# Two-block transformer step on one core: late expert rows set aside early in memory, with three smaller moves to GpSimd and SyncE

## The chip, the cores and the metric

The kernel runs on one core of a Trainium2 chip. Five engines take instructions: TensorE (PE; PEld loads its weights), VectorE (DVE), ScalarE (ACT), GpSimd (POOL) and SyncE (SP, which here issues most DMAs). The metric is the device time of one launch in microseconds, lower is better.

## The reference

Two transformer blocks follow each other on 2048 tokens of 1024 features, all in float32. The first has latent attention beside a state-space layer. The second has attention beside retention, and then a mixture of 32 experts of which each token takes two. The parts that the change touches compute this:

```python
mixed = jnp.concatenate([attn, ssm], axis=-1) @ w_out[l]
x = x + _rms_norm(mixed, post_norm_g[l])                       # end of block 1 (mixing 1)
...
cross = jnp.einsum('bhnik,nbhkv,hi->bhniv', qc, s_prev, xi)    # retention: queries times a decay xi
...
pcounts = (counts + MOE_BLOCK - 1) // MOE_BLOCK * MOE_BLOCK    # rows of each expert, up to a multiple of 128
buf_tok = jnp.full((P,), T, jnp.int32).at[dest].set(tok_s)     # token of each row
xb = h_pad[buf_tok].reshape(nblk, MOE_BLOCK, D)                # the rows, in blocks of 128
def expert_block(args):
    x_blk, e = args
    return (jax.nn.silu(x_blk @ w_gate[e]) * (x_blk @ w_up[e])) @ w_down[e]
yb = lax.map(expert_block, (xb, blk_e)).reshape(P, D)
```

The rows of an expert are its tokens, gathered from `h`. There are at least 32 blocks of 128 rows (2 x 2048 / 128) and at most 63, since each expert's last block is filled up. With these inputs 46 blocks are used.

## The kernel before

The work runs in stages, each a function with a program for every engine: block 1's attention, state-space layer and mixing (`mix_1`), then projection 2, attention 2, retention, mixing 2, dispatch, experts and combine. The order on each engine is the order in which its program is written; waits on semaphores join the engines. A DMA that SP issues goes on a hardware queue (q1), one that POOL issues as an indirect gather on a software queue (q0).

Experts. A row of this text is the work between the transposes of one block and those of the next. In a row PE transposes the next block's rows (L3766, `e_pT` from `w_XG`), multiplies by gate, up and down weights split in a high and a low part (three products each), and transposes the hidden block. ACT makes the high parts of the weights (L3831), DVE the low parts (L3879: `down_low`, `up_low`, `gate_low`, each 128x4096). SP loads the weights of a block (L3713, 2 MB each; one that has not changed is skipped, so an expert with two blocks loads once) and stores the result (L3717, `between_yb`). In SP's `tile`, the load of gate for block i+2 is the last thing; it waits until `gate_low` has been made. POOL does only one thing: `gather` (L3474) fetches the 128 rows of block i from `between_h` by an indirect DMA, with the list `M["slots"]`, into one of the two buffers `w_XG`, as soon as PE has transposed block i-2 (`t_ps` at i-1):

```python
for i in range(2, NB + 2):
    pool.wait_ge(S["t_ps"], i - 1)
    pool.wait_ge(x_loaded[i % 2], 16 * (i // 2))
    gather(pool, D, M, i)
```

The loop runs over all 64 block numbers, though only some are used: `tiles_in_use` (L82) counts pairs of blocks and skips those not in use, and in a skipped pair SP raises `t_ps` by 2 (`skipped`), which lets POOL run on through the gathers of empty blocks. Their list holds numbers out of bounds, so nothing is fetched. SP also loads the residual (`load_residual`) after the loop. POOL waits for its last gather before the stage ends and combine starts.

Mixing 1. For each of 16 token tiles DVE scales the product (`X`, L1992), later adds the old x to it (`add_x`, L1997), and between them makes `CS` (L2059), from which ACT makes `CH` and then, behind a table load, a tanh that DVE waits for. POOL sums squares of pairs (L1914, L1918), and PE waits for the sum.

Retention. For each of 4 heads DVE runs 15 steps of the state (L3086), makes `QX`, the queries times their decay (`queries`, L3098), and then the decayed scores (L3103) from products of PE. POOL clears memory and is then free.

Of the kernel before, what the change touches and what calls it, by code (L numbers as in the profile page):

```python
# [80 lines left out]

def tiles_in_use(eng, least, most, pairs_in_use, body, skipped_pair=None):  # L82

    body(tile_at(0))
    body(tile_at(1))
    pairs = eng.value_load(pairs_in_use, min_val=least, max_val=most)
    with eng.Fori(0, most) as j:
        with eng.If(j < pairs):
            body(Tile(2 * j + 2, 0, j + 1))
            body(Tile(2 * j + 3, 1, j + 1))  # L90
        if skipped_pair:
            with eng.Else():
                skipped_pair(j)
    return pairs
# [1764 lines left out]
def mix_1(nc, I, D, C, M):  # L1859
# [7 lines left out]
    with ExitStack() as ctx:  # L1867
# [40 lines left out]
        @block.gpsimd  # L1908
        def _(pool):
            k.clear_spent(pool)  # L1910

            def tile(t):
                pool.wait_ge(S["sq_ready"], t.i + 1)
                pool.tensor_tensor(sq_pairs[:], sq[:, 0:SM // 2, :], sq[:, SM // 2:SM, :], ALU.add).then_inc(S["sq_halved"], 1)  # L1914
                pool.wait_ge(S["sq_halved"], t.i + 1)
                if not t.first:
                    pool.wait_ge(S["norm_ps"], t.i)
                pool.tensor_tensor(sq_sum[:], sq_pairs[:, 0, :], sq_pairs[:, 1, :], ALU.add).then_inc(S["sq_summed"], 1)  # L1918

            tiles(pool, NT, tile)  # L1920

        @block.sync
# [56 lines left out]
        def _(dve):  # L1979
# [13 lines left out]

            def add_x(t):
                dve.wait_ge(S["tmp_ready"], t.i + 1)
                dve.wait_ge(x_loaded[t.b], 16 * t.n + 16)
                dve.tensor_tensor(X1[t.b][:], X1[t.b][:], XT[t.b][:], ALU.add).then_inc(S["x1_ready"], 1)  # L1997

            def gelu_inner(t):
# [20 lines left out]
            def tile(t):  # L2020
# [57 lines left out]
            last_stage(tile_at(NT - 1))  # L2078
            add_x(tile_at(NT - 1))

# [494 lines left out]
def attention_2(nc, I, C, D, M):  # L2575
# [14 lines left out]
    with ExitStack() as ctx:  # L2590
# [22 lines left out]
        names = """v_loaded v_ones k_zeros k_rows k_split k_high q_zeros q_high_act q_top q_high q_split max_ps maxed top_ready row_ps row_ready  # L2613
            v_high v_low p_high p_low p_low_dve s_ps p_ready o_ps rec_ready o_ready zeros_ready yb_zeroed
            decay_loaded expo_loaded neg_ready e_ready l_ready lg_ready cols_ready decay_ready decay_step""".split()
# [6 lines left out]
        @block.sync  # L2622
        def _(sp):
            def load_query(i):
                src = D["qka"][0:QA, :].rearrange("(h p) t -> p h t", p=HD)[:, :, i * P:(i + 1) * P]
                for half in range(2):
                    sp.dma_start(RQ[i % 2][half * HD:(half + 1) * HD], src).then_inc(q_loaded[i % 2], 16)

            def load_keys(g):
                for half in range(2):  # L2630
                    sp.dma_start(KX[g][half * HD:(half + 1) * HD, :], D["qka"][QA + g * HD:QA + (g + 1) * HD, :]).then_inc(k_loaded[g], 16)

            load_query(0)
            load_keys(0)
            load_keys(1)
            for g in range(HKV):
                sp.dma_start(V1[:, :, g, 0:HD], D["va"].rearrange("(n p) d -> p n d", p=P)[:, :, g * HD:(g + 1) * HD]).then_inc(S["v_loaded"], 16)
            load_query(1)
            sp.dma_start(ecol[:], I["ret_ecol"]).then_inc(S["expo_loaded"], 16)
            sp.dma_start(expo[:], I["ret_expo"]).then_inc(S["expo_loaded"], 16)  # L2640
            sp.dma_start(R["KT0"][:].rearrange("p n d -> p (n d)"), D["krt"][0:P, :]).then_inc(R["keys_loaded"], 16)
            sp.wait_ge(S["zeros_ready"], 1)
            for n in range(SURE, NB + 1):
                sp.dma_start(D["yb"][n * P:(n + 1) * P, :], zeros[:]).then_inc(S["yb_zeroed"], 16)
            for i in range(NT):
                if i + 2 < NT:
                    sp.wait_ge(S["q_split"], i + 1)
                    load_query(i + 2)
                sp.wait_ge(S["o_ready"], HKV * (i + 1))
                sp.dma_start(D["ao2"].rearrange("(h p) t -> p h t", p=HD)[:, :, i * P:(i + 1) * P], OT[i % 2][:]).then_inc(stored[i % 2], 16)  # L2650
            for b in range(2):
                sp.wait_ge(stored[b], 16 * (NT // 2))
            sp.wait_ge(S["yb_zeroed"], 16 * (NB + 1 - SURE))

# [251 lines left out]
def retention(nc, I, D, C, M):  # L2906

    with ExitStack() as ctx:
# [36 lines left out]
        def _(pool):  # L2945
            pool.memset(K_[HD:P, :], 0.0).then_inc(S["k_zeros"], 1)
            k.clear_spent(pool)

        @block.sync
# [131 lines left out]
        def _(dve):  # L3081
# [10 lines left out]

            def queries(h):
                dve.wait_ge(q_loaded[h % 2], 32 * (h // 2 + 1))
                if h:
                    dve.wait_ge(S["o_ps"], GRP * h)
                q = Q[h % 2][:].rearrange("p (n i) -> p n i", i=P)
                dve.tensor_tensor(QX[:], q, bcast(XI[:, h:h + 1, :], [P, NT, P]), ALU.mult).then_inc(S["qx_ready"], 1)  # L3098

            def decayed(h):  # L3100
# [563 lines left out]
def experts(nc, I, D, C, M):  # L3664

    with ExitStack() as ctx:
# [13 lines left out]
        pD = k.ps("pD", (P, 2, BANK))  # L3680
        names = "turn t_ps xt_high xt_low g_ps u_ps th_ready silu_ready hh_ready ht_ps ht_high ht_low d_ps y_ready".split()
# [3 lines left out]
        x_loaded, stored = M["rows_gathered"], [k.sem(f"stored{b}") for b in range(2)]  # L3685
        block = ctx.enter_context(nc.Block())
# [5 lines left out]
        def after(t):  # L3692
            return Tile(t.i + 1, 1 - t.b, t.n + t.b)

        def raw(n, t):
# [6 lines left out]
        def _(sp):  # L3702
# [44 lines left out]
            wait(w_low["down"], last.i + 1)  # L3747
            for b in range(2):
                wait(stored[b], 16 * pairs + 32)

        @block.gpsimd
        def _(pool):
            k.clear_spent(pool)
            for i in range(2, NB + 2):
                pool.wait_ge(S["t_ps"], i - 1)
                pool.wait_ge(x_loaded[i % 2], 16 * (i // 2))
                gather(pool, D, M, i)
            pool.wait_ge(x_loaded[0], 16 * (NB // 2 + 2))
            pool.wait_ge(x_loaded[1], 16 * (NB // 2 + 1))

        @block.tensor
        def _(pe):
            def transposed(t):
                pe.wait_ge(x_loaded[t.b], 16 * t.n + 16)
                for c in range(KC):
# [32 lines left out]

            def tile(t):
                i = t.i  # L3800
# [5 lines left out]
                if not t.first:  # L3806
                    hidden_transposed(t.before())
                pe.wait_ge(S["xt_low"], i + 1)
                transposed(after(t))
                gate_up(t, pG, "gate", XL, WH)  # L3810
# [9 lines left out]

            pe.sem_inc(S["d_ps"], 1)
            transposed(tile_at(0))
            last = last_in_use(tiles_in_use(pe, *in_use, tile))
            hidden_transposed(last)
# [185 lines left out]
def block_pair_kernel(nc, I, out):  # L4010

    D = {}
    for name, rows, cols in (
# [3 lines left out]
        ("qka", QA + KA, SEQ + CTX), ("qkr", 2 * RQ, SEQ + CTX), ("ao2", QA, SEQ), ("ret", HR * P, NT * RV), ("x2", SEQ, DM),  # L4017
        ("h", SEQ, DM), ("yb", (NB + 1) * P, DM), ("tv", NT * P, GB * POWERS * GC), ("tu", NT * P, GB * POWERS * GC),
        ("w_in_2", DM, PROJ), ("w_out", DM, DM), ("w2h", DM, DM), ("w2l", DM, DM), ("hh", DM, DM * 2), ("hl", DM, DM * 2), ("cos", NT * P, HG * NCH), ("sin", NT * P, HG * NCH),
    ):  # L4020
        D[name] = nc.dram_tensor("between_" + name, [rows, cols], F32, kind="Internal").ap()
    with ExitStack() as ctx:
# [15 lines left out]
        with ExitStack() as projection:  # L4038
# [20 lines left out]
            project_2(nc, I, D, C, M)  # L4059
        M["logits"] = k.sb("logits", [P, NT, NL])  # L4060
        M["weights"] = k.sb("weights", [P, 2, NT])
# [4 lines left out]
        M["pairs_in_use"] = k.sb("pairs_in_use", [P, 1], I32)  # L4066
        M["constants"] = {n: k.sb(n, shape) for n, shape in zip(DISPATCH_CONSTANTS, DISPATCH_SHAPES)}
        M["constants_loaded"] = k.sem("constants_loaded")
# [121 lines left out]
```

## Time and profile before

| what | value |
| --- | --- |
| median of 3 runs | 4377.21 us (4375.51 to 4379.54) |
| the profiled execution: its time, its span | 4377.03 us, 4375.2 us |
| PE, DVE, ACT, POOL busy | 92%, 68%, 56%, 28% of the span |
| mixing 1 | about 1385 to 1668 us |
| retention | about 2997 to 3125 us |
| dispatch ends, experts begin | about 3410 us |
| experts end, combine begins | about 4290 us |

The profile shows one execution. In a timeline row stand the start and the length in us, the engine, the line, the operation, its output and inputs, how many instructions are joined in it, and in brackets how long the engine had been idle before and who released it. SPq and ACTq are DMAs issued on those engines' queues. In a row of windows stand the stretch, its length, the busy time of each engine with its number of instructions, then TensorE's granted clock as a share of full speed, the share of time that the DMA engines were busy, and GB/s.

### The profile page before, as it was taken

The numbers are of one execution on the slowest core, as the hardware profiler recorded it, in microseconds if no ns is written. First come the engines' busy times: TensorE is split into PE (matmuls) and PEld (weight loads), VectorE is DVE, ScalarE is ACT, GpSimd is POOL, SyncE is SP. The second block draws the span as 40 slices with busy tenths as digits, with TensorE's granted clock in tenths as the row PEclk, the third lists the DMA queues.
The fourth block names the chain that finished last, engine by engine and source line by source line (L and its number), as shares of the span: only waits on it lengthen the run. The fifth ranks groups of instructions, "written<-read, shape, count | busy, mean of one in ns | idle before, by whom it ended". The sixth has DMA issues, their size and how long they took to land. (4 is left out here: it accounts for less than half of the span.)

```text
span 4375.2 us, 61240 instructions
## 1 busy us (share of the span) xinstructions
PE 4016.5 (92%) x21445; PEld 3410.6 (78%) x21445; DVE 2986.3 (68%) x3835; ACT 2431.7 (56%) x3867; POOL 1211.5 (28%) x842
## 2 busy tenths in 40 slices
PE   8989799999997997999799999996697799999985
PEld 8978688898776786888588888886586688888872
DVE  6667555555486885444477777775655799999975
ACT  7634333333313554333388888886422577777763
POOL 0000145445310110000288888882000111111114
PEclk9999899999998998999799999998898899999997
DMA  6667733334496433222430000005543688888976
GB/s 229 219 211 243 228 106 118 102 111 124 148 276 189 142 110 114 70 71 72 121 134 15 22 15 15 15 10 181 173 144 111 239 309 327 326 322 337 379 304 276
DMA packets 417337, 728.63 MB, mean 167 GB/s; under 512 B 121744, under 2 KB 314384, under 8 KB 396304
## 3 DMA queue, kind: packets, MB, share of 16 engines
q1 hardware_dynamic: 389040, 665.61, 44.2%
q0 software_dynamic: 13968, 33.58, 2.0%
q10 hardware_dynamic: 14160, 27.27, 2.0%
q8 instruction: 95, 1.56, 0.2%
q14 instruction: 74, 0.61, 0.0%
HBM read 603.93 MB, written 213.91 MB: 187 GB/s over the span
## 5 line engine op out<-in xcount | busy, mean ns | idle before, releaser
L2675 POOL TENSOR_TENSOR a_PL<-a_PT,a_PH 128x512 fp32r<-128x512 f32 x512 | 674.9, 1333 | 132.1 <-ACT a_PH L2794 128.9
L2844 DVE TENSOR_REDUCE a_part<-a_pA 128x1 f32<-128x1024 f32 (+1 forms) x384 | 360.0, 955 | 95.2 <-PE a_pA L2698 90.8
L2792 ACT ACTIVATE a_PT<-a_pB 128x512 f32<-128x512 f32 x576 | 340.8, 592 | 78.6 <-PE a_pB L2721 77.3
L2794 ACT ACTIVATE a_PH<-a_PT 128x512 fp32r<-128x512 f32 x576 | 364.4, 633 | 18.3
L3474 POOL DMA_INDIRECT w_XG<-between_h,all_slots x65 | 119.9, 1845 | 786.6 <-PE e_pT L3766 705.6
L1397 ACT ACTIVATE a_PT<-a_pT 128x512 f32<-128x512 f32 x128 | 69.6, 595 | 408.7 <-PE a_pT L1327 408.7
L1432 DVE TENSOR_REDUCE a_maxima<-a_pS 128x1 f32<-128x512 f32 x256 | 176.1, 689 | 130.0 <-PE a_pS L1309 128.6
L1341 PE MATMUL a_pO<-a_V,a_PT 128*128 128x128 f32 x2048 | 250.4, 276 | 1.0 <-DVE a_PT L1445 1.0
L1341 PEld LDWEIGHTS a_pO<-a_V,a_PT 128*128 128x128 f32 x2048 | 244.2, 192 | 6.8 <-DVE a_PT L1445 1.6
L1239 POOL TENSOR_TENSOR a_QL<-a_RQ,a_QT 128x512 fp32r<-128x512 f32 x16 | 20.6, 1288 | 797.5 <-DVE a_QP L1467 797.5
L2739 PE MATMUL a_pO<-a_PL,a_VH 128*128 128x512 f32 x576 | 225.6, 392 | 3.1 <-DVE a_PL L2854 2.1
L2733 PE MATMUL a_pO<-a_PH,a_VH 128*128 128x512 f32 x576 | 228.1, 396 | 0.0
L2720 PE MATMUL a_pB<-a_QA,a_KH 128*128 128x512 f32 x576 | 225.8, 392 | 1.1 <-ACT a_QA L2767 0.7
L2734 PE MATMUL a_pO<-a_PH,a_VL 128*128 128x512 f32 x576 | 225.8, 392 | 0.0
L2721 PE MATMUL a_pB<-a_QA,a_KL 128*128 128x512 f32 x576 | 225.2, 391 | 0.0
L3879 DVE TENSOR_TENSOR e_gate_low<-w_gate,e_gate_high 128x4096 fp32r<-128x4096 f32 x47 | 207.8, 4421 | 16.1 <-ACT e_gate_high L3831 16.1
L2698 PE MATMUL a_pA<-a_KH,a_QA 128*128 128x512 f32 (+1 forms) x640 | 198.6, 377 | 19.1 <-ACT a_KH L2781 15.6
L3831 ACT ACTIVATE e_up_high<-w_up 128x4096 fp32r<-128x4096 f32 x46 | 167.3, 3638 | 77.0 <-DMA w_up<-in_moe_w_up 69.4
L3879 DVE TENSOR_TENSOR e_down_low<-w_down,e_down_high 128x4096 fp32r<-128x4096 f32 x46 | 203.3, 4419 | 0.8 <-ACT e_down_high L3831 0.7
L3879 DVE TENSOR_TENSOR e_up_low<-w_up,e_up_high 128x4096 fp32r<-128x4096 f32 x46 | 203.1, 4416 | 0.0
L3831 ACT ACTIVATE e_gate_high<-w_gate 128x4096 fp32r<-128x4096 f32 x47 | 170.7, 3632 | 56.1 <-SPq L3721 34.9
L3831 ACT ACTIVATE e_down_high<-w_down 128x4096 fp32r<-128x4096 f32 x46 | 167.3, 3636 | 16.0 <-DMA w_down<-in_moe_w_down 15.8
(651 smaller groups left out, 10601.2 us busy)
## 6 DMA issues: line engine op xcount, KB each, us to landing
w_gate<-in_moe_w_gate SPq DMA_DIRECT2D x48, 2048.0 KB, 7.5
w_up<-in_moe_w_up SPq DMA_DIRECT2D x47, 2048.0 KB, 12.1
w_down<-in_moe_w_down SPq DMA_DIRECT2D x46, 2048.0 KB
between_yb<-e_Y SPq DMA_DIRECT2D x45, 512.0 KB, 7.3
a_row_w<-in_w_ada SPq DMA_DIRECT2D x16, 1024.0 KB, 5.4
between_x<-m_X SPq DMA_DIRECT2D x32, 512.0 KB, 2.7
between_yb<-a_zeros SPq DMA_DIRECT2D x32, 512.0 KB, 14.0
between_tv<-pz_OV SPq DMA_DIRECT2D x16, 576.0 KB, 2.9
```

Of the source, the lines that this page charges most:

```text
L1341: mm = pe.matmul(pO[:, 0:dv], PT[:, jj, :], values(V, h, jj), start=jj == 0, stop=jj == key_tiles - 1)
L2675: pool.tensor_tensor(PL[:, t % RING, :], PT[:, t % RING, :], PH[:, t % RING, :].bitcast(F32), ALU.subtract).then_inc(S["p_low"], 1)
L2720: pe.matmul(pB[t % 2][:], KH[g][:, tile], QA1[i % 2][:, heads, :], start=True, stop=False)
L2721: pe.matmul(pB[t % 2][:], KL[g][:, tile], QA2[i % 2][:, heads, :], start=False, stop=True).then_inc(S["s_ps"], 1)
L2733: pe.matmul(pO[u % 2][:], VH[:, j, g, :], high, start=first, stop=False)
L2734: pe.matmul(pO[u % 2][:], VL[:, j, g, :], high, start=False, stop=False)
L2739: pe.matmul(pO[u % 2][:], VH[:, j, g, :], low, start=False, stop=last).then_inc(S["o_ps"], 1)
L2792: act.activation(PT[:, t % RING, :], pB[t % 2][:], ACT.Exp, scale=scale).then_inc(S["p_ready"], 1)
L2794: act.activation(PH[:, t % RING, :], PT[:, t % RING, :], ACT.Copy).then_inc(S["p_high"], 1)
L2844: dve.tensor_reduce(part[:, h, r % (NG2 // G4):r % (NG2 // G4) + 1], src, AX_X, ALU.max).then_inc(S["maxed"], 1)
L3831: act.activation(WH[n][:], raw(n, t)[:], ACT.Copy).then_inc(w_high[n], 1)
L3879: dve.tensor_tensor(WL[n][:], raw(n, t)[:], WH[n][:].bitcast(F32), ALU.subtract).then_inc(w_low[n], 1)
```

## The change

Experts. The first 32 blocks are now run without a test (SP, PE and the others loop over 15 pairs after the first two blocks), and the pairs after them under the test as before. POOL gathers only blocks 2 to 32 into `w_XG`. After each of these gathers it gathers one block of the 33rd to 63rd (`set_aside`) into one buffer, `all_spare`, which held the logits and the constants of dispatch before. SP stores that buffer to a new table in memory, `between_hs` (`store_aside`, at the head of its tile), before POOL may fill it again. In late tiles SP loads the rows of a block from that table into `w_XG` (`load_aside`), and PE waits on SP's semaphore there. SP no longer raises `t_ps` for skipped pairs. Two blocks at the end of the table are filled with zeros during attention 2.

Mixing 1 and retention. `add_x` moves from DVE to POOL, behind POOL's sums of the next tile; `queries` moves from DVE to POOL, with waits for the queries, for the products of the head before and for its own `QX` before.

```diff
-def tiles_in_use(eng, least, most, pairs_in_use, body, skipped_pair=None):
+def tiles_in_use(eng, least, most, pairs_in_use, body, late_body=None, between=None):
     body(tile_at(0))
     body(tile_at(1))
     pairs = eng.value_load(pairs_in_use, min_val=least, max_val=most)
-    with eng.Fori(0, most) as j:
+    with eng.Fori(0, least) as j:
+        body(Tile(2 * j + 2, 0, j + 1))
+        body(Tile(2 * j + 3, 1, j + 1))
+    if between:
+        between()
+    late_body = late_body or body
+    with eng.Fori(least, most) as j:
         with eng.If(j < pairs):
-            body(Tile(2 * j + 2, 0, j + 1))
-            body(Tile(2 * j + 3, 1, j + 1))
-        if skipped_pair:
-            with eng.Else():
-                skipped_pair(j)
+            late_body(Tile(2 * j + 2, 0, j + 1))
+            late_body(Tile(2 * j + 3, 1, j + 1))
...
@@ mix_1, POOL
+                if not t.first:
+                    add_x(t.before())
+
+            def add_x(t):
+                pool.wait_ge(S["tmp_ready"], t.i + 1)
+                pool.wait_ge(x_loaded[t.b], 16 * t.n + 16)
+                pool.tensor_tensor(X1[t.b][:], X1[t.b][:], XT[t.b][:], ALU.add).then_inc(S["x1_ready"], 1)
...
@@ mix_1, DVE
                 dve.tensor_tensor(CS[:], a[:], bcast(r2[:].unsqueeze(1), [P, SM, P]), ALU.mult).then_inc(S["cs_ready"], 1)
-                if not t.first:
-                    add_x(t.before())
...
@@ attention 2, SP
+            for n in range(ASIDE, ASIDE + 2):
+                sp.dma_start(D["hs"][n * P:(n + 1) * P, :], zeros[:]).then_inc(S["hs_zeroed"], 16)
...
@@ retention, POOL
+            def queries(h):
+                pool.wait_ge(q_loaded[h % 2], 32 * (h // 2 + 1))
+                if h:
+                    pool.wait_ge(S["o_ps"], GRP * h)
+                    pool.wait_ge(S["qx_ready"], h)
+                else:
+                    pool.wait_ge(S["k_zeros"], 1)
+                q = Q[h % 2][:].rearrange("p (n i) -> p n i", i=P)
+                pool.tensor_tensor(QX[:], q, bcast(XI[:, h:h + 1, :], [P, NT, P]), ALU.mult).then_inc(S["qx_ready"], 1)
...
@@ retention, DVE
             for h in range(HR):
                 states(h)
-                queries(h)
                 decayed(h)
...
+FIRST_ASIDE = SURE + 1
+ASIDE = NB - SURE
...
@@ experts
+        def set_aside(pool, n):
+            if n:
+                pool.wait_ge(S["aside_stored"], 16 * n)
+            pool.indirect_dma_start(out=M["spare"][:], out_offset=None, in_=D["h"],
+                                    in_offset=bass.IndirectOffsetOnAxis(ap=M["slots"][:, FIRST_ASIDE + n:FIRST_ASIDE + n + 1], axis=0),
+                                    bounds_check=SEQ - 1, oob_is_err=False).then_inc(S["aside_gathered"], 16)
...
-            def skipped(j):
-                wait(S["t_ps"], 2 * j + 3)
-                sp.sem_inc(S["t_ps"], 2)
-
-            pairs = tiles_in_use(sp, *in_use, tile, skipped)
+            def store_aside(n):
+                wait(S["aside_gathered"], 16 * n + 16)
+                sp.dma_start(D["hs"][ds(n * P, P), :], M["spare"][:]).then_inc(S["aside_stored"], 16)
+
+            def load_aside(block, b):
+                sp.dma_start(XG[b][:], D["hs"][ds((block - FIRST_ASIDE) * P, P), :]).then_inc(x_loaded[b], 16)
+
+            def early_tile(t):
+                if not isinstance(t.i, int):
+                    store_aside(t.i - 2)
+                tile(t)
...
+            def late_tile(t):
+                wait(S["t_ps"], t.i + 1)
+                load_aside(t.i + 2, t.b)
+                tile(t)
...
+            pairs = tiles_in_use(sp, *in_use, early_tile, late_tile, first_aside)
...
-            for i in range(2, NB + 2):
+            for i in range(2, FIRST_ASIDE):
                 pool.wait_ge(S["t_ps"], i - 1)
-                pool.wait_ge(x_loaded[i % 2], 16 * (i // 2))
+                pool.wait_ge(x_gathered[i % 2], 16 * (i // 2))
                 gather(pool, D, M, i)
+                set_aside(pool, i - 2)
```

How the instructions stand on POOL in the experts stage, before (ISA rows are waits and other instructions without a tile; `w_XG` are the two buffers of rows, `between_h` the tokens' features):

```order
L112 ISA x17
L3474 DMA w_XG<-between_h,all_slots 128x1024 x63
L3666 UNCONDITIONAL_BRANCH
L3943 UNCONDITIONAL_BRANCH
L3949 DMA c_Y<-between_yb,all_dest 128x1024
```

and after the change:

```order
L116 ISA x17
L3488 DMA w_XG<-between_h,all_slots 128x1024
L3712 DMA all_spare<-between_h,all_slots 128x1024
L3488 DMA w_XG<-between_h,all_slots 128x1024
L3712 DMA all_spare<-between_h,all_slots 128x1024
```

The run of 63 gathers became 31 pairs of a gather into `w_XG` and one into `all_spare`; the second of a pair waits for SP's store of the buffer, and the next gather into `w_XG` stands behind it.

On SP, at the border between two tiles of the early blocks, before (with the loads of block numbers that decide what is fetched):

```order
L3713 DMA w_gate0<-in_moe_w_gate 128x4096
L3708 TENSOR_LOAD all_block_expert
L3708 ISA x2
L3710 REGISTER_ALU
L3710 TENSOR_LOAD all_block_new
L3710 ISA x2
L3713 ISA
L3713 DMA w_down0<-in_moe_w_down 128x4096
```

and after:

```order
L3734 DMA w_gate0<-in_moe_w_gate 128x4096
L1858 ISA
L3755 DMA between_hs<-all_spare 128x1024
L3729 TENSOR_LOAD all_block_expert
L3729 ISA x2
L3731 REGISTER_ALU
L3731 TENSOR_LOAD all_block_new
L3731 ISA x2
L3734 ISA
L3734 DMA w_down0<-in_moe_w_down 128x4096
```

The wait (L1858) and the store of the spare buffer came between the load of the gate weights of one tile and the load of the down weights of the next, on the same queue.

On POOL in mixing 1, in the body of the loop over tiles, before:

```order
L1914 TENSOR_TENSOR m_sq_pairs<-m_sq 128x256
L1917 REGISTER_ALU
L1918 TENSOR_TENSOR m_sq_sum<-m_sq_pairs 128x128
L1913 REGISTER_ALU
L1914 TENSOR_TENSOR m_sq_pairs<-m_sq 128x256
```

and after:

```order
L1918 TENSOR_TENSOR m_sq_pairs<-m_sq 128x256
L1921 REGISTER_ALU
L1922 TENSOR_TENSOR m_sq_sum<-m_sq_pairs 128x128
L1929 ISA
L1930 TENSOR_TENSOR m_X<-m_X,m_XT 128x1024
```

The addition of 128x1024 stands between the sum of one tile and the squares of the next.

## Rows read from the trace of the kernel before

**Rows 1.** The page's head: span of the profiled execution and its instructions.

```profile
span 4375.2 us, 61240 instructions
```

**Rows 2.** Windows in experts: stretch, length, busy (count) by engine, clock, DMA share, GB/s.

```profile
3462.60:4100.70 638.10, 637.90 (x3026) 531.57 (x3025) 592.67 (x253) 494.51 (x252) 75.16 (x36) 1.00 0.85 326
4118.90:4193.10 74.20, 71.97 (x338) 58.80 (x337) 65.92 (x29) 54.83 (x28) 9.35 (x4) 1.00 0.99 386
```

**Rows 3.** Timeline of PE, transposes of one block: start, length, operation.

```profile
3515.70 1.04 PE L3766 MATMUL e_pT<-all_ident,w_XG 128*128 128x128 f32 x8
```

**Rows 4.** Timeline of DVE in the row of that block.

```profile
3514.32 4.42 DVE L3879 TENSOR_TENSOR e_down_low<-w_down,e_down_high 128x4096 fp32r<-128x4096 f32 x1
...
3520.36 4.42 DVE L3879 TENSOR_TENSOR e_up_low<-w_up,e_up_high 128x4096 fp32r<-128x4096 f32 x1
...
3525.67 4.42 DVE L3879 TENSOR_TENSOR e_gate_low<-w_gate,e_gate_high 128x4096 fp32r<-128x4096 f32 x1
```

**Rows 5.** Timeline of SP's queue in that row and the start of the next.

```profile
3519.09 0.33 SPq L3713 DMA_DIRECT2D w_down<-in_moe_w_down  x1
...
3530.54 0.34 SPq L3713 DMA_DIRECT2D w_gate<-in_moe_w_gate  x1
```

**Rows 6.** Timeline of POOL, in that row.

```profile
3517.53 2.08 POOL L3474 DMA_INDIRECT w_XG<-between_h,all_slots  x1 [15.54 <-PE e_pT L3766]
```

**Rows 7.** Timeline of POOL, near the stage's end.

```profile
4245.70 4.55 POOL L3474 DMA_INDIRECT w_XG<-between_h,all_slots  x1 [0.30 <-issue]
```

**Rows 8.** Timeline of DVE, near the stage's end.

```profile
4244.96 4.42 DVE L3879 TENSOR_TENSOR e_down_low<-w_down,e_down_high 128x4096 fp32r<-128x4096 f32 x1
```

**Rows 9.** Line L3717, SP's stores of a block's result: issue to landing.

```profile
DMA to landing us min/median/max: 2.6/7.3/8.4
```

**Rows 10.** Line L3474, POOL's gathers: issue to landing.

```profile
DMA to landing us min/median/max: 2.1/9.0/12.6
```

**Rows 11.** Windows of PE at the second row: stretch, length, busy, clock, DMA share, GB/s.

```profile
3439.60:3443.30 3.70, 0.58 (x5) 1.00 0.40 71
3443.30:3446.70 3.40, 3.40 (x14) 0.50 0.91 376
```

**Rows 12.** Timeline of the stage's end and combine's start, all engines.

```profile
4256.99 0.40 ACTq L3871 DMA_DIRECT2D between_yb<-e_Y  x1
...
4282.58 0.99 POOL L3474 DMA_INDIRECT w_XG<-between_h,all_slots  x1 [0.30 <-issue]
...
4290.34 1.86 ACT L3966 ACTIVATE c_diagonal<-all_ident,all_weights 128x128 f32<-128x128 f32 x6 [33.55 <-PEq L3666]
```

**Rows 13.** Line L3871, ACT's store of the last block: issue to landing.

```profile
DMA to landing us min/median/max: 8.6/8.6/8.6
```

**Rows 14.** Groups of POOL's lines: form, count, busy us, mean ns, idle before.

```profile
L1262 POOL TENSOR_TENSOR a_ada_t<-a_ada_w,all_cs 128x2048 f32<-128x2048 f32 x16 | 58.0, 3624 | 22.5 <-PE a_pC L1364 19.8 <-POOL a_QP L1241 2.4
...
L1267 POOL TENSOR_TENSOR a_ada_t<-a_ada_t 128x1024 f32<-128x1024 f32 x16 | 39.0, 2440 | 1.3
```

**Rows 15.** Timeline of DVE in one tile of mixing 1.

```profile
1565.03 1.28 DVE L1992 SCALAR_TENSOR_TENSOR m_X<-m_pM,m_r_m,m_post_g 128x1024 f32<-128x1024 f32 x1
...
1567.96 0.69 DVE L2059 TENSOR_TENSOR m_CS<-m_a,m_r 128x512 f32<-128x512 f32 x1 [0.19 <-DVE m_r L2054]
1568.57 1.22 DVE L1997 TENSOR_TENSOR m_X<-m_X,m_XT 128x1024 f32<-128x1024 f32 x1
...
1571.92 0.69 DVE L2025 SCALAR_TENSOR_TENSOR m_thg<-m_thg,m_GS 128x512 f32<-128x512 f32 x1 [1.54 <-ACT m_tha L2102]
```

**Rows 16.** Line L2018 of DVE: ns min/median/max, first and last start.

```profile
L2018 DVE SCALAR_TENSOR_TENSOR m_v<-m_th,m_yh x16: 693/1226/1234, 1380.9 to 1628.1; 128x512 f32<-128x512 f32 x16
```

**Rows 17.** Waits of PE, 1395 to 1650 us: us in total, times, longest.

```profile
PE m_pN L2188 <- POOL m_sq_sum L1918: 7.3, 7, 1.2
```

**Rows 18.** Timeline of DVE in retention's first head.

```profile
3016.57 2.29 DVE L3098 TENSOR_TENSOR r_QX<-r_Q,rt_XI 128x2048 f32<-128x2048 f32 x1
```

**Rows 19.** Timeline of PE in retention's third head.

```profile
3070.65 5.61 PE L3200 MATMUL r_pX<-r_Q,r_K 128*128 128x128 f32 x31 [7.35 <-DMA r_K<-between_qkr]
```

More of the change, by code:

```diff
@@ L1 @@
+import itertools
 import math
@@ L1918, in tile @@
                 pool.tensor_tensor(sq_sum[:], sq_pairs[:, 0, :], sq_pairs[:, 1, :], ALU.add).then_inc(S["sq_summed"], 1)
+                if not t.first:
[4 more added lines that the diff above has]
+                pool.tensor_tensor(X1[t.b][:], X1[t.b][:], XT[t.b][:], ALU.add).then_inc(S["x1_ready"], 1)
             tiles(pool, NT, tile)
+            add_x(tile_at(NT - 1))
         @block.sync
@@ L1992, in last_stage @@
                 dve.scalar_tensor_tensor(X1[b][:], pM[:].rearrange("p a b -> p (a b)"), r_m[:], post_g[:], ALU.mult, ALU.mult).then_inc(S["tmp_ready"], 1)
[L1994 to L1997, printed above, removed]
             def gelu_inner(t):
@@ L2652, in _ @@
                 sp.wait_ge(stored[b], 16 * (NT // 2))
+            sp.wait_ge(S["hs_zeroed"], 32)
             sp.wait_ge(S["yb_zeroed"], 16 * (NB + 1 - SURE))
@@ L2947, in _ @@
             k.clear_spent(pool)
+            def queries(h):
[7 more added lines that the diff above has]
+                pool.tensor_tensor(QX[:], q, bcast(XI[:, h:h + 1, :], [P, NT, P]), ALU.mult).then_inc(S["qx_ready"], 1)
+            for h in range(HR):
+                queries(h)
         @block.sync
@@ L3091, in states @@
                         dve.wait_ge(S["states_run"], GRP * h + n // 4 + 1)
[L3093 to L3098, printed above, removed]
             def decayed(h):
@@ L3680, in experts @@
         pD = k.ps("pD", (P, 2, BANK))
-        names = "turn t_ps xt_high xt_low g_ps u_ps th_ready silu_ready hh_ready ht_ps ht_high ht_low d_ps y_ready".split()
+        names = "turn t_ps xt_high xt_low g_ps u_ps th_ready silu_ready hh_ready ht_ps ht_high ht_low d_ps y_ready aside_gathered aside_stored".split()
         S = {n: k.sem(n) for n in names}
@@ L3684, in experts @@
         w_loaded = {n: [k.sem(f"w_loaded_{n}{b}") for b in range(len(W[n]))] for n in kinds}
-        x_loaded, stored = M["rows_gathered"], [k.sem(f"stored{b}") for b in range(2)]
+        x_gathered, x_loaded, stored = M["rows_gathered"], [k.sem(f"x_loaded{b}") for b in range(2)], [k.sem(f"stored{b}") for b in range(2)]
         block = ctx.enter_context(nc.Block())
@@ L3730, in tile, with first_aside @@
                 load("gate", Tile(i + 2, t.b, t.n + 1), i + 2)
-            def skipped(j):
-                wait(S["t_ps"], 2 * j + 3)
-                sp.sem_inc(S["t_ps"], 2)
-            pairs = tiles_in_use(sp, *in_use, tile, skipped)
+            def store_aside(n):
[7 more added lines that the diff above has]
+                tile(t)
+            def first_aside():
+                store_aside(ASIDE - 1)
+                wait(S["aside_stored"], 16 * ASIDE)
+                wait(S["t_ps"], FIRST_ASIDE - 1)
+                load_aside(FIRST_ASIDE, FIRST_ASIDE % 2)
+            def late_tile(t):
+                wait(S["t_ps"], t.i + 1)
+                load_aside(t.i + 2, t.b)
+                tile(t)
+            for b in range(2):
+                sp.sem_inc(x_loaded[b], 16 * (SURE // 2 + 1 - b))
+            pairs = tiles_in_use(sp, *in_use, early_tile, late_tile, first_aside)
             last = last_in_use(pairs)
@@ L3748, in _ @@
             for b in range(2):
+                wait(x_loaded[b], 16 * pairs + 32)
                 wait(stored[b], 16 * pairs + 32)
@@ L3753, in _ @@
             k.clear_spent(pool)
-            for i in range(2, NB + 2):
+            for i in range(2, FIRST_ASIDE):
                 pool.wait_ge(S["t_ps"], i - 1)
-                pool.wait_ge(x_loaded[i % 2], 16 * (i // 2))
+                pool.wait_ge(x_gathered[i % 2], 16 * (i // 2))
                 gather(pool, D, M, i)
-            pool.wait_ge(x_loaded[0], 16 * (NB // 2 + 2))
-            pool.wait_ge(x_loaded[1], 16 * (NB // 2 + 1))
+                set_aside(pool, i - 2)
+            pool.wait_ge(x_gathered[0], 16 * (SURE // 2 + 1))
+            pool.wait_ge(x_gathered[1], 16 * (SURE // 2))
         @block.tensor
@@ L3797, in down, with gathered, loaded_aside, tile @@
                 product(HTL, WH, last=True).then_inc(S["d_ps"], 1)
-            def tile(t):
+            def gathered(t):
+                pe.wait_ge(x_gathered[t.b], 16 * t.n + 16)
+            def loaded_aside(t):
+                pe.wait_ge(x_loaded[t.b], 16 * t.n + 16)
+            def tile(t, rows_known=gathered):
                 i = t.i
@@ L3808, in tile @@
                 pe.wait_ge(S["xt_low"], i + 1)
+                rows_known(after(t))
                 transposed(after(t))
@@ L3821, in _ @@
             pe.sem_inc(S["d_ps"], 1)
+            gathered(tile_at(0))
             transposed(tile_at(0))
-            last = last_in_use(tiles_in_use(pe, *in_use, tile))
+            last = last_in_use(tiles_in_use(pe, *in_use, tile, lambda t: tile(t, loaded_aside)))
             hidden_transposed(last)
@@ L4059, in block_pair_kernel @@
             project_2(nc, I, D, C, M)
-        M["logits"] = k.sb("logits", [P, NT, NL])
+        M["spare"] = k.sb("spare", [P, DM])
+        M["logits"] = M["spare"][:, 0:NT * NL].rearrange("p (t n) -> p t n", n=NL)
         M["weights"] = k.sb("weights", [P, 2, NT])
@@ L4066, in block_pair_kernel @@
         M["pairs_in_use"] = k.sb("pairs_in_use", [P, 1], I32)
-        M["constants"] = {n: k.sb(n, shape) for n, shape in zip(DISPATCH_CONSTANTS, DISPATCH_SHAPES)}
+        ends = list(itertools.accumulate((shape[1] for shape in DISPATCH_SHAPES), initial=NT * NL))
+        M["constants"] = {n: M["spare"][:, lo:hi] for n, lo, hi in zip(DISPATCH_CONSTANTS, ends, ends[1:])}
         M["constants_loaded"] = k.sem("constants_loaded")
```

6 lines of the change are left out of this document (2 added, 4 removed).

## Prediction

> **What bounds the kernel now.** I read the page's head first: the profiled execution's span is 4375.2 us [rows 1], its time 4377.03, so 1.8 us lie around the span and the sum below is made against 4377.0, which is also the median of the runs (4377.21). Then the windows of the experts, the stage in which most of the change lies. Over 36 rows PE is busy 637.90 of 638.10 us [rows 2], 17.7 us a row: PE is the bound, at granted clock 1.00 (2.4 GHz), and nothing else has to be late for more than a moment before PE stands. DVE is close behind (592.67), and the DMA engines are busy 0.85 of the time. Where several blocks in a row load all their weights the DMA share is 0.99 at 386 GB/s, and four rows take 74.20 us, 18.55 each [rows 2]. So there are two margins to watch, PE's and the DMAs'. POOL is nearly idle, with one gather to a row. The timelines of one row then show when everything happens in it. Times below are counted from the transposes that begin the row, 3515.70 [rows 3]; the next row begins at 17.7.
>
> DVE makes `down_low` from -1.4 to 3.0, `up_low` from 4.7 to 9.1 and `gate_low` from 10.0 to 14.4 [rows 4]. SP loads down at 3.4 and gate at 14.8 [rows 5]. POOL's gather begins at 1.8 [rows 6]; it is for the block two rows on, so it has 34 us to land in and takes 9.0 at the median, 12.6 at most [rows 10]. Its cover is large.
>
> **A gather waits for VectorE.** The last thing read is how long POOL takes to issue a gather. Alone it takes 0.99 us [rows 12]. The one at 4245.70 takes 4.55 us, to 4250.25 [rows 7]; DVE's `down_low` runs from 4244.96 to 4249.38 [rows 8], so it ended 0.9 us behind the DVE instruction that had begun before it. The one at 1.8 ends at 3.9, again 0.9 behind `down_low` [rows 4, 6]. I take it that a gather which begins beside a DVE instruction with two inputs in SBUF ends 0.9 us after that instruction. The Trainium skill (SBUF — State Buffer, Who interferes with whom) has the exclusive lock on a port pair that this looks like, but says that a `tensor_tensor` on VectorE was not seen to stall a DMA issued by GpSimd. By that sentence no gather would be held and the result would be rival A below; the 4.55 us beside a `tensor_tensor` speak against it here.
>
> **Experts, early rows.** In an early row POOL now issues two gathers in this order: the set-aside of block n, which waits until SP's store of block n-1 has landed, and behind it the gather of block n+3, which PE needs at the end of that same row n+2. SP's store stands behind the load of gate in SP's order and in the queue. So it is issued at about 14.9 of row n+1 [rows 5] and lands 2.6 to 8.4 us later, 7.3 at the median, if it fares as the stores of results on the same queue do [rows 9]. That is -0.2 of row n+2 at the least (gate skipped, nothing ahead in the queue), 4.5 at the median, 5.6 at the most. The gather that had 34 us now has what is left of one row behind two issues by POOL. Three cases follow.
>
> At -0.2 the set-aside waits out `down_low`, ends at 3.9, and the gather goes behind it, just ahead of `up_low` or held by it to 10.0. From POOL's end a gather lands 6.9 us later (9.0 less 2.1) at the median, 10.5 at the most [rows 6, 10]: at 11 to 17, or at the most at 20.5. Mostly in time. Between 3.0 and 4.7 DVE is free, the set-aside passes in 1 us, the gather is held by `up_low` to 10.0 and lands at 17 to 20.5: late by about 1 us in the mean. From 4.7 on the set-aside is held by `up_low` to 10.0, and by then `gate_low` has begun, which holds the gather to 15.3; it lands at 22.2 at the median, 25.8 at the most. PE then stands 4.5 us, up to 8.
>
> A row that stands gives the time back to the ring: the next store is issued at its usual place while the row has become longer, so the next request meets the first case. About 0.7 of the blocks load new weights (32 experts on 46 blocks), and behind a load comes the late case. The set-asides of blocks 0 to 28 have a gather behind them, so 29 rows can be late; I take every second, 14: ten at 4.5 us and four at 1 us, **+49**. The bounds are 0 (every request early) and 29 x 8 = 230; nearest to the rows is the alternation.
>
> A standing PE also costs clock. At the second row PE was busy for 0.58 of 3.70 us, and in the 3.4 us after it the granted clock was 0.50, the lower level of 1.2 GHz [rows 11]: 1.7 us lost. Not every gap will do it; four of the ten give **+6** (0 to 24).
>
> DMA bytes: the early rows get 31 stores of 0.52 MB, and 13 gathers of 0.52 MB (blocks 33 to 45; the lists of the others are empty) that stood in the late rows: 23 MB, which would take 60 us at 386 GB/s [rows 2] with nothing beside it. The early rows have 0.15 of 17.7 x 31 us free, 82 us, so it fits in the mean. Rows that load three weights are full already. **+5** (0 to 30).
>
> SP's wait for the set-aside has the loads of down and up behind it. With a set-aside that ends at 10.0 and lands by 17 to 20.5, SP goes on before 3.4 of the next row, which is 21.1 [rows 5]; it costs nothing. The loop without a test changes nothing on PE, which has no idle time for it in the 36 rows. The late rows load from the table two rows ahead, by SP: 0. The two zero stores in attention 2 follow 32 others there that nothing waits on: 0.
>
> **Experts, the end.** Before, POOL issues gathers of empty blocks until 4282.58, and combine begins only at 4290.34 [rows 12], while ACT had stood 33.55 us. These gathers are gone. What then ends last is the store of the last block, issued 4256.99 and landed 8.6 us later, 4265.6 [rows 12, 13]. From the last gather's start to combine's were 7.8 us, some 2 of them until it landed, so combine comes about 5.6 after: 4271.2, **-19**. The residual loads on SP no longer wait behind skipped pairs and are not later than before. Bounds -25 to -10.
>
> **Mixing 1.** DVE loses 1.22 us a tile, but stands 1.54 us for ACT's tanh right after it [rows 15]; that gain is 0. On POOL an addition of this form takes 2.44 us [rows 14]. It begins when X is scaled, 1566.31, and ends at 1568.8, so it lies over the start of `CS` at 1567.96, which has two inputs in SBUF. The multiplication `m_v` takes 0.69 us at the first tile, but 1.23 at the median [rows 16], when POOL sums beside it: DVE waits for POOL as POOL does for DVE. So `CS` comes 0.9 later and with it the whole chain to POOL's sum of squares, for which PE already waits 7 times in these 255 us [rows 17], in every second tile. 7 x 0.9 and something at the edges: **+7** (0, when nothing is held, to 15 x 0.9 = 14).
>
> **Retention.** 4 x 2.29 us leave DVE [rows 18]; on POOL they take 3.62 each [rows 14], beside the 15 steps of the state. In the third head PE stands 7.35 us for a load, `r_K` [rows 19], and takes up what the first two heads saved; the last two can keep up to 4.6, less about 0.7 each where POOL holds DVE's first step. **-3** (-9 to +3).
>
> Sum: 4377.0 + 49 + 6 + 5 - 19 - 3 + 7 = **4422 us**, slower. Its own range is 4395 to 4455.
>
> **Rivals.** A: the gathers land in time, since they slip in between two DVE instructions or are not held. For it speaks that the early case has room; against it the 2.08 us of nearly every gather in the steady rows. Experts' early rows cost 0 to 5: 4377 - 19 - 3 + 7 + 0 to 5 = 4362 to 4367, faster. B: most requests fall into the free slot from 3.0 to 4.7; the median landing, 4.5, lies in it. 14 rows at 1 us, no clock lost: 4377 + 14 + 5 - 15 = 4381. C: the full rows are the bound; half of the 60 us of added bytes cannot be hidden and the stores land later, so the late case is the rule: +30 more, 4452. It decides as soon as the DMA share of the early rows is at 0.97 or more. D: the end does not come earlier, since the residual loads and the last store stand behind late loads of weights: +19, 4441.
>
> **How the numbers follow.** Forecast 0.55, A 0.17, B 0.13, C 0.10, D 0.05. What a measurement of this kernel can tell from no change is 0.2%, 8.8 us. A is faster but for its edge, B within it for the most part, the rest is slower: faster 0.18, same 0.09, slower 0.73. The range takes in A but its lower edge and C: 4360 to 4462.
>
> **What would show it.** In the profile of the changed kernel: early rows of 17.7 and of 20 to 24 us in turn; PE waiting on `w_XG` by DMA, some 55 us in all in early rows; POOL's gathers of 4 to 5 us ending 0.9 behind DVE's; DMA share of the early rows near 0.93; the late rows at 17.7 as before; combine about 15 us behind the last matmul instead of 35; in mixing 1 `CS` longer or later by 0.9. I am wrong if POOL's gather of block n+3 is issued before 5 in most rows, or if PE stands in fewer than 8 of them.

## The result, and the profile after

The changed kernel takes 4417.9 us in the median (4412.8 to 4423.9, four runs) against 4378.4 before: 1.0094 times as long, with a 95% interval of 1.0082 to 1.0105. The profiled execution is the shortest of the four, 4412.84 us with a span of 4410.6, 35.4 longer than the span before [rows 1]. One execution of those in this document, one of the eight of the first experiment, took 8591.0 us and is left out of that run's ratio. The stages, read from both traces by the first and last instruction of their tiles:

| stage (us) | before | after | difference |
| --- | --- | --- | --- |
| from 1342.5 us, late in block 1's state-space part, to attention 2 (mixing 1 and projection 2 in it) | 810.9 | 818.6 | +7.7 |
| attention 2 | 843.5 | 842.7 | -0.8 |
| retention, to PE's last product of scores | 106.5 | 105.2 | -1.3 |
| rest of retention, mixing 2 and dispatch | 313.3 | 312.0 | -1.3 |
| experts, first transposes to the last result | 840.1 | 894.9 | +54.8 |
| from there to combine's first instruction | 33.5 | 8.2 | -25.3 |
| combine | 84.9 | 86.5 | +1.6 |

The early rows first. These are windows of 29 rows (the fourth to the 32nd, counted from one) and of twelve late ones in the changed kernel; columns as in [rows 2].

```profile
3463.60:4026.20 562.60, 527.47 (x2439) 437.28 (x2437) 480.15 (x204) 397.47 (x204) 154.02 (x58) 0.97 0.85 326
4073.50:4287.90 214.40, 213.65 (x1010) 176.83 (x1009) 197.77 (x85) 165.20 (x85) 0.00 (x0) 1.00 0.94 371
```

and this is the window of the same 29 rows before:

```profile
3462.60:3976.50 513.90, 513.70 (x2438) 428.27 (x2437) 477.47 (x204) 398.05 (x204) 60.55 (x29) 1.00 0.83 319
```

The rows grew by 48.7 us. PE stood 35.1 of them (562.60 less 527.47), and its same 2438 matmuls took 13.8 longer, at a mean granted clock of 0.97 instead of 1.00. The late rows, which load from the table, run at 17.9 each. What PE waited for in the experts of the changed kernel (total us, times, longest):

```profile
PE e_pT L3809 <- DMA w_XG<-between_h,all_slots: 35.1, 15, 6.6
...
PE e_pT L3809 <- DMA w_XG<-between_hs: 9.6, 1, 9.6
```

The first line is the forecast wait, in 15 rows. The second was not forecast: the first late block came 9.6 us late from the table.

One of the worst rows shows the chain. Its first transposes, two issues on SP's queue in the row before, GpSimd's timeline in it, and VectorE's:

```profile
3864.02 1.09 PE L3809 MATMUL e_pT<-all_ident,w_XG 128*128 128x128 f32 x8 [0.57 <-DMA w_XG<-between_h,all_slots]
```

```profile
3859.28 0.34 SPq L3734 DMA_DIRECT2D w_gate<-in_moe_w_gate  x1
3859.90 0.36 SPq L3755 DMA_DIRECT2D between_hs<-all_spare  x1
```

```profile
3872.01 1.09 POOL L3712 DMA_INDIRECT all_spare<-between_h,all_slots  x1 [17.59 <-issue]
3873.41 5.21 POOL L3488 DMA_INDIRECT w_XG<-between_h,all_slots  x1 [0.30 <-issue]
```

```profile
3867.83 4.42 DVE L3930 TENSOR_TENSOR e_up_low<-w_up,e_up_high 128x4096 fp32r<-128x4096 f32 x1
...
3873.33 4.43 DVE L3930 TENSOR_TENSOR e_gate_low<-w_gate,e_gate_high 128x4096 fp32r<-128x4096 f32 x1
```

PE's transposes at the end of the row:

```profile
3888.52 1.76 PE L3809 MATMUL e_pT<-all_ident,w_XG 128*128 128x128 f32 x7 [6.61 <-DMA w_XG<-between_h,all_slots]
```

The store of the block set aside before was issued at 3859.90, behind a load of gate at 3859.28, and landed 11.0 us later, at 6.9 of the row. The set-aside of the next block, waiting for that, began at 8.0, beside `up_low`, and ended 0.85 us behind it. The gather that PE needed began 0.08 us after `gate_low` and was held until 14.6, 0.9 behind `gate_low`. It landed 15.1 us after its start, and PE stood 6.6. This is the forecast's third case, step by step, with a store that landed later than the forecast's 5.6 of the row at the most.

The clock in the end of that wait and behind it (PE alone, columns as in [rows 11]):

```profile
3882.00:3888.50 6.50, 0.00 (x0) 0.66 1.02 390
3888.50:3891.90 3.40, 3.38 (x12) 0.50 1.01 434
3891.90:3895.30 3.40, 3.40 (x11) 0.65 0.97 414
3895.30:3898.70 3.40, 3.40 (x16) 1.00 0.89 364
```

The two windows after the wait lose 1.7 and 1.2 us.

The end of the stage, which answers to [rows 12], on ACT:

```profile
4316.09 0.40 ACTq L3922 DMA_DIRECT2D between_yb<-e_Y  x1
4324.13 2.15 ACT L4017 ACTIVATE c_diagonal<-all_ident,all_weights 128x128 f32<-128x128 f32 x7 [8.24 <-PEq L3680]
```

The store landed 7.7 us after its issue, at 4323.8, and combine began 0.3 us later.

Mixing 1, line L2067 (`CS`, before L2059) and PE's waits from 1395 to 1650 us, which answer to [rows 15, 17]:

```profile
L2067 DVE TENSOR_TENSOR m_CS<-m_a,m_r x16: 693/1394/1502, 1402.7 to 1657.1; 128x512 f32<-128x512 f32 x16
```

```profile
PE m_pN L2193 <- POOL m_sq_sum L1922: 11.6, 12, 2.0
```

`CS` takes 1.39 us in the median where it took 0.69, and PE waits for the sum of squares 12 times instead of 7, 11.6 us instead of 7.3.

### The profile page after: what moved, and what is told of

Same layout as the page of the kernel before. It is cut to its first block and busy times, and to the rows that moved or that the text cites. A ratio compares the mean times of both kernels' runs of the same rounds, so it can differ in the third digit from the quotient of the medians.

```text
span 4410.6 us, 61260 instructions
## 1 busy us (share of the span) xinstructions
PE 4032.1 (91%) x21445; PEld 3422.2 (78%) x21445; DVE 2968.6 (67%) x3815; ACT 2431.5 (55%) x3867; POOL 1314.7 (30%) x861
## 5 line engine op out<-in xcount | busy, mean ns | idle before, releaser
L3712 POOL DMA_INDIRECT all_spare<-between_h,all_slots x31 | 53.5, 1727 | 435.8 <-DMA between_hs<-all_spare 367.5
L1409 ACT ACTIVATE a_PR<-a_pS,a_bias 128x512 f32<-128x512 f32 x256 | 172.9, 702 | 3.4 <-DVE a_bias L1443 3.4
```

## The experiments

The theory: a gather on GpSimd is held by a VectorE instruction with two inputs in SBUF, and the ring of one buffer (filled by a gather, stored, filled again) puts two such gathers one behind the other into the row at whose end the second is needed. The rivals: the added bytes are the bound; or the gain at the end needs the table. Each run is compared with runs of the kernel before on the same chip (4376.9 or 4375.6 us in the median).

**No two-input instruction beside the gathers.**

```diff
-                dve.tensor_tensor(WL[n][:], raw(n, t)[:], WH[n][:].bitcast(F32), ALU.subtract).then_inc(w_low[n], 1)
...
+                dve.tensor_tensor(by_bank(WL[n]), by_bank(raw(n, t)), bcast(pZ[:].unsqueeze(1), [P, KC * DE // BANK, BANK]), ALU.subtract).then_inc(w_low[n], 1)
```

(`pZ` is a bank of zeros in PSUM, TensorE's memory for results; `by_bank` views a tile in pieces of a bank. What this kernel leaves out is the split of the weights: its low parts are the weights themselves, so it does not compute the reference.)

> The changed kernel, but VectorE makes the low parts of the weights from the weights and a bank of zeros in PSUM, so that no 128x4096 instruction has two inputs in SBUF; the low parts are then the weights themselves and the output is not the reference's. Theory (GpSimd's two issues are held by VectorE's two-input instructions): every gather takes about 1.0 us, block n+3 is requested by 3 to 10 of its row, PE's waits for gathered rows fall from 35 us to under 10, the 9.6 us before the first late block stay at 5 to 10: 4380 to 4395 us. Rival (the stores and the added bytes fill the queues, and a long GpSimd instruction is only a symptom): the waits stay above 25 us, 4405 to 4420.

Measured: 4386.8 us (ratio to before 1.0026, 1.0015 to 1.0037), 31 less than the change. Its groups of GpSimd and VectorE (count, busy us, mean ns, idle before):

```profile
L3488 POOL DMA_INDIRECT w_XG<-between_h,all_slots x33 | 32.9, 997 | 55.2 <-issue 41.7 <-PE e_pT L3810 13.4
L3713 POOL DMA_INDIRECT all_spare<-between_h,all_slots x31 | 30.7, 992 | 502.3 <-DMA between_hs<-all_spare 445.0 <-PE e_pT L3810 33.7 <-issue 23.6
```

```profile
L3932 DVE TENSOR_TENSOR e_up_low<-w_up,e_pZ 128x4096 fp32r<-128x4096 f32 x46 | 202.9, 4411 | 0.0
```

and PE's waits:

```profile
PE e_pT L3810 <- DMA w_XG<-between_h,all_slots: 10.7, 8, 2.6
PE e_pT L3810 <- DMA w_XG<-between_hs: 9.3, 1, 9.3
```

VectorE's instructions are as long as before (4.41 us) and as many; only the second input moved from SBUF to PSUM. Every gather now takes 0.99 us. So it is the second SBUF input that holds the gather, and it is worth 24 of the 35 us of waits. The other 10.7 are left with the order on GpSimd and the ring as they were.

**The gather ahead of the set-aside.**

```diff
                 gather(pool, D, M, i)
-                set_aside(pool, i - 2)
+                if i > 2:
+                    set_aside(pool, i - 3)
+            set_aside(pool, ASIDE - 1)
```

> The changed kernel with the order on GpSimd turned round: the gather of block n+3 stands ahead of the set-aside of block n, not behind it. Bytes, stores and waits are the same. Theory (the ring of one buffer holds up the gather behind it): the gather has a whole row more, PE's waits in early rows fall from 35 us to under 3, with them some 10 us of lower clock; the wait of 9.6 us before the first late block stays: 4370 to 4382 us. Rival (added bytes are the bound in full rows): waits stay above 20 us, 4400 to 4420.

Measured: 4370.8 us (0.9985, 0.9976 to 0.9995), 47 less than the change and a little under the kernel before. The 29 early rows, GpSimd's group and PE's one wait for rows:

```profile
3464.70:3980.60 515.90, 514.24 (x2438) 428.05 (x2437) 478.23 (x204) 397.27 (x204) 135.85 (x57) 1.00 0.91 355
```

```profile
L3488 POOL DMA_INDIRECT w_XG<-between_h,all_slots x33 | 103.9, 3150 | 67.8 <-issue 41.4 <-PE e_pT L3811 26.4
```

```profile
PE e_pT L3811 <- DMA w_XG<-between_hs: 9.4, 1, 9.4
```

The gathers are still held, 3.15 us in the mean, and nobody waits for them any more: 515.9 us where the change took 562.6 and the kernel before 513.9. The added bytes are all there (355 GB/s against 319), so here they cost about 2 us. The rival on the bytes falls; its sign, a DMA share of 0.97 in the early rows, was not there either (0.85 in the changed kernel, 0.91 here).

**The store ahead of the load of gate.**

```diff
                     store(t.before())
+                if aside:
+                    store_aside(i - 1)
                 load("gate", Tile(i + 2, t.b, t.n + 1), i + 2)
...
```

(`aside` is set in all early tiles but the first; the store at the head of a tile and the one behind the early rows are gone.)

> The changed kernel, but SyncE stores the set-aside block ahead of the load of gate, not behind it; the order on GpSimd is left as it is. Theory (half of the lateness is the store's place behind a 2 MB load): the store is issued at 12 to 13 of a row and lands 2.6 to 5 us later, the set-aside is requested before the row begins and passes with or just behind down_low, the gather is issued by 5: PE's waits in early rows fall from 35 us to under 8, the wait before the first late block to 3 to 8: 4370 to 4388 us. Rival (the two issues on GpSimd are held for 9 to 10 us wherever the request falls): waits stay above 25 us, 4405 or more.

Measured: 4402.5 us (1.0065, 1.0049 to 1.0080). PE's waits:

```profile
PE e_pT L3808 <- DMA w_XG<-between_h,all_slots: 20.3, 13, 2.6
...
PE e_pT L3808 <- DMA w_XG<-between_hs: 7.5, 1, 7.5
```

Neither side had this: the waits fell by 15 us, to 20.3, all short. GpSimd's gathers, all of the stage (ns):

```profile
L3488 POOL DMA_INDIRECT w_XG<-between_h,all_slots x33: 986/4624/5140, 3416.7 to 3996.5; - x33
```

The gather starts at 4 to 5 of a row as I expected, but 22 of the 29 in the early rows are held, nearly all by `up_low`: the gather takes 4.6 us in the median, and lands 9.9 us after GpSimd's end instead of the 6.9 that I had taken. An early request only moves the second issue from behind `gate_low` to behind `up_low`.

**The end of the stage alone, in the kernel before.**

```diff
-            for i in range(2, NB + 2):
+            def fetch(i):
                 pool.wait_ge(S["t_ps"], i - 1)
                 pool.wait_ge(x_loaded[i % 2], 16 * (i // 2))
                 gather(pool, D, M, i)
-            pool.wait_ge(x_loaded[0], 16 * (NB // 2 + 2))
-            pool.wait_ge(x_loaded[1], 16 * (NB // 2 + 1))
...
+            for i in range(2, 2 * least + 3):
+                fetch(i)
+            for j in range(least, most):
+                with pool.If(pairs > j):
+                    fetch(2 * j + 3)
+                    fetch(2 * j + 4)
```

(GpSimd's two waits for its last gathers go with the empty ones, and SP's `skipped` is gone.)

> The kernel before, with one edit: GpSimd gathers the blocks beyond the 32nd only under a test whether they are used, and SyncE no longer runs them through; nothing is set aside. Theory (combine waited only for the empty gathers): combine starts 8 to 10 us behind the last block's result, 4350 to 4356 us, 23 to 27 less than before, and early and late rows as before. Rival (the early table is needed for it, or the residual loads end the stage): a gain under 10 us, 4368 or more.

Measured: 4351.5 us (0.9944, 0.9929 to 0.9959). ACT at the end:

```profile
4253.98 0.40 ACTq L3874 DMA_DIRECT2D between_yb<-e_Y  x1
4262.27 1.86 ACT L3969 ACTIVATE c_diagonal<-all_ident,all_weights 128x128 f32<-128x128 f32 x6 [8.48 <-PEq L3666]
```

The 25 us come without any table. The rival falls.

**Mixing 1 alone**, in the kernel before: the change's lines for `add_x` and no others.

> The kernel before with the part in mixing 1 alone: the addition of the old x on GpSimd. Theory (VectorE's CS is held for 0.7 to 0.9 us by the addition, and the chain to the sum of squares bounds a tile): PE's wait for the sum grows from 7 to 16 us, 4383 to 4387 us. Rival (PE bounds the stage, the chain has slack): within 2 us of before.

Measured: 4388.7 us (1.0027, 1.0016 to 1.0039), 11.8 more, above the range I gave; the interval reaches from 7 to 17. `CS` and PE's waits:

```profile
L2063 DVE TENSOR_TENSOR m_CS<-m_a,m_r x16: 692/1392/1498, 1402.5 to 1656.9; 128x512 f32<-128x512 f32 x16
```

```profile
PE m_pN L2189 <- POOL m_sq_sum L1918: 11.7, 12, 2.0
```

Both are those of the changed kernel, and the stage is 7.6 us longer (818.5 against 810.9). This profile's span is 10.5 us longer than the one before; the other 2.9 lie in retention (109.4), and no line of the edit bears on that. I leave it open.

**Retention alone**, in the kernel before: the change's `queries` and no other lines.

> The kernel before with the part in retention alone: the queries times decay on GpSimd. Theory (VectorE is on the path of the last two heads, and loads set the first ones): 1 to 4 us less than before. Rival (GpSimd's multiplication, 4.5 us in the changed kernel's profile, is as late as VectorE's 2.3 were): within 1 us, or 1 to 3 us more.

Measured: 4373.8 us (0.9997, 0.9988 to 1.0006): no difference that can be told. The stage, as in the table, is 103.9 us long, and 103.6 to 105.2 in the seven profiles with the edit, against 105.6 to 109.4 in the three without it. A gain of some 2 to 3 us fits both; the times neither show it nor exclude it.

**The end and retention together**, the last two edits.

> The kernel before with the tested gathers of the run on the end of the stage (nothing set aside) and with the part in retention. Theory: both gains add, 4345 to 4352 us. Rival (the part in retention gives nothing): as without it, 4349 to 4355 us.

Measured: 4353.4 us (0.9949, 0.9935 to 0.9962), the same as the end alone within both intervals.

**The table, mended.** The gather ahead of the set-aside; block 33 (counted from 0, as in the code) gathered by GpSimd like those before it, so that 30 blocks are set aside and SP no longer stores, waits and loads between the early and the late rows; mixing 1 as before.

```diff
-FIRST_ASIDE = SURE + 1
-ASIDE = NB - SURE
+FIRST_ASIDE = SURE + 2
+ASIDE = NB - SURE - 1
...
-                set_aside(pool, i - 2)
+                if 3 <= i < SURE:
+                    set_aside(pool, i - 3)
+            set_aside(pool, ASIDE - 1)
...
```

> The changed kernel with its table kept and its losses mended: the gather of a block ahead of the set-aside of three blocks before; the 33rd block gathered by GpSimd like those before it, so that 30 blocks are set aside and the first load from the table is that of the 34th; mixing 1 as it was before. Theory (the two waits and mixing 1 are all that the change costs): no wait for rows over 1 us, 4346 to 4354 us, 64 to 70 less than the change. Rival (the 23 MB of added transfers cost by themselves): 4358 or more, with early rows at 17.9 or longer.

Measured: 4351.8 us (0.9947, 0.9931 to 0.9962), 66 less than the change. The early rows and the late ones:

```profile
3454.20:3974.60 520.40, 514.73 (x2438) 427.86 (x2437) 478.77 (x204) 396.32 (x204) 123.20 (x58) 1.00 0.90 351
3992.30:4225.30 233.00, 230.97 (x1094) 191.79 (x1093) 214.39 (x92) 178.75 (x92) 0.00 (x0) 1.00 0.94 373
```

PE's wait for the first late block is gone, and so are the long ones for gathered rows. The early rows are 6.5 us longer than before (520.4 against 513.9), and ACT waited 22.5 us in them for loads of gate where it had waited 9.5. So the added transfers probably cost something after all, though less than the rival had; the run with the gather ahead has the same loads' wait at 20.9 and lost 2.0, and one profile of each does not settle the size. The whole equals the end alone. Both beat the kernel before by 24 to 25 us and the change by 66; the end alone is the simpler one.

## Why the prediction was right

Slower, by the mechanism named, at 4417.9 us against 4422. That the sum came so close is in part luck: its terms were less good, and their errors cancelled. Two of the signs that I had named were weak: the DMA share of the early rows was 0.85, not 0.93, and the gather was issued before 5 in 14 of the 29 rows, one short of the "most" that was to prove me wrong.

- *Early rows, +49.* Measured 35.1. The count was right (15 rows for 14), the size was not: three rows waited over 5 us, five 1.9 to 3.6, seven under 1.4. Of the 29 gathers nine were held by `gate_low` (25.8 of the 35.1 us are behind these), eleven by `up_low`, and nine slipped in and took 1 us. Against that SP's stores landed 8.9 us after their issue in the median (12.3 at most), not 7.3 (8.4), and the gathers 8.2 after GpSimd's end in the median, not 6.9.
- *Clock, +6.* Measured 13.8 on the same matmuls of the 29 rows. I let four gaps cost 1.7 each. The longest wait cost 2.9 in the rows shown above, and shorter ones cost too: 1.2 behind one of 2.1 us (last section).
- *Bytes, +5.* In the changed kernel they do not show apart from the waits; the early rows lost about 2 us with the order on GpSimd turned round and 6.5 in the mended table.
- *SP's waits, 0.* This step failed. I had SP go on in time because nothing behind the store was late. But between the early and the late rows SP has to store the last block set aside, wait until it has landed, and only then load block 33. In SP's timeline of the changed kernel:

```profile
4041.17 0.35 SPq L3755 DMA_DIRECT2D between_hs<-all_spare  x1
4050.26 1.30 SPq L3758 DMA_DIRECT2D w_XG<-between_hs  x2
```

  The store stands behind gate at 15.0 of the row, lands 8.9 us later, and the row of 17.7 is over before the load is issued. It cost 9.6 us and some 2 of clock. `first_aside` was in the diff; I read it as part of the late rows, which load two rows ahead.
- *The end, -19.* Measured -25.3. I took 5.6 us between the last landing and combine as fixed. In the changed kernel combine starts 0.3 us after the last landing, and with the empty gathers alone taken away 8.3 us after the last store's issue. So the 5.6 went with the empty gathers: GpSimd stood 7.4 us behind the last of them, though its landing in the records is at 2.1 us.
- *Mixing 1, +7.* Measured 7.7 up to attention 2, and 7.6 with that part alone; here too the size is partly luck. `CS` did not start later behind the instruction before it; it lasted 0.7 us longer, which is the same for the chain. PE's waits for the sum grew by only 4.3 us. The same 1376 matmuls also took 5.1 us longer, at a lower mean clock, and the forecast had no clock in this term; and projection 2, which the edit does not touch, took 2.6 us less. PE in mixing 1, before and after (columns as in [rows 11]):

```profile
1381.70:1661.20 279.50, 259.46 (x1376) 0.98 0.37 127
1381.70:1670.40 288.70, 264.59 (x1376) 0.96 0.36 123
```

  These matmuls took 261.7 to 264.9 us in the five profiles with this edit, 259.3 to 262.4 in the five without it, and projection 2 took 481.6 to 484.7 in all ten.
- *Retention, -3.* Measured -1.3 in the stage. GpSimd's multiplication took 4.5 us, not 3.62, and PE did not wait for it.
- *Given nothing.* The first three rows took 42.5 us instead of 45.9, and the twelve late ones 214.4 instead of 216.8. The end alone, which leaves both as they were, has 42.6 and 219.5, so differences of this size come without the table.

Rival A was not wrong about room in the early case, as the rows without a wait show. Its ground, that VectorE's `tensor_tensor` does not hold a gather, is refuted by the first experiment. The Trainium skill (SBUF — State Buffer, Who interferes with whom) says, beside the sentence that the prediction names, that a VectorE instruction with two SBUF inputs contends with a GpSimd instruction that reads SBUF. The gathers agree with that: 0.99 us in the median with one such input, 4.6 with two. The sentence on `tensor_tensor` does not hold for these gathers. Whether it is the list of rows that a gather reads from SBUF was not tested.

## What to carry to other kernels

Where one buffer is filled, emptied and filled again by two queues, put the transfer that somebody waits for ahead of the one that waits for the buffer: the same work in the other order was worth 47 us here. Before moving work to an idle engine, look at what its instructions can be held by and at how much lead its results had; GpSimd was busy for 60 of the 514 us of the early rows, but each of its issues hung on VectorE's timetable, which only an early request had hidden. And where a gain at a stage's end comes packed with a rebuilt loop, run the end alone first.

## What the runs showed that I had not expected

- A wait of 2.1 us, before the row at 3483.6, was followed by 3.4 us at a mean clock of 0.66, while the row at 3522.8, behind a wait as long (2.07), ran at 1.00 from its start:

```profile
3483.60:3487.00 3.40, 3.40 (x15) 0.66 1.05 451
3522.80:3526.20 3.40, 3.39 (x19) 1.00 0.70 196
```

- A gather of an empty list at the end of the kernel before has a recorded landing 2.1 us after its start, but GpSimd stood 7.4 us behind the last one before combine:

```profile
4290.99 0.95 POOL L3949 DMA_INDIRECT c_Y<-between_yb,all_dest  x1 [7.42 <-POOLq L3666]
```

  How long such a gather takes until its semaphore rises can't be read from its landing.
